# The last quarter of each low half, made by GpSimd in the last expert block

## The reference, cut to what matters

```
logits = xf @ router_w                       # (256, 8)
top_logit, top_idx = top_k(logits, 2); gates = softmax(top_logit)
# tokens sorted by expert into padded blocks of 128 rows
yb = (silu(xb @ w_gate[e]) * (xb @ w_up[e])) @ w_down[e]     # one block xb, expert e; w_gate (1024, 3584)
x  = x + sum over the token's two experts of yb[row] * gate
out = rms_norm(x)
```

## Time and profile before

| | us |
|---|---|
| median of 3 runs | 1396.18 (1395.97 to 1396.36) |
| the profiled execution, own time | 1393.4 |
| its span, first to last instruction | 1391.1 |
| TensorE busy | 1372.3 (99%) |
| VectorE busy | 1145.6 (82%) |
| ScalarE busy | 938.1 (67%) |
| GpSimd busy | 41.4 (3%) |
| HBM traffic over the span | 322 GB/s |
| `w_lo` instructions on VectorE (L390), 401 | 914.7 |

### The profile page before, as it was taken

The page is one execution under the profiler, slowest core; times in us unless marked ns, Lnnn a source line. Parts: engine busy times, 40 slices in busy tenths (PEclk is TensorE's granted clock), DMA queues, the critical chain, the costliest instruction groups (busy, mean ns, idle before and its releaser), DMA issues.

```text
span 1391.1 us, 19149 instructions
## 1 busy us (share of the span) xinstructions
PE 1372.3 (99%) x7313; PEld 1170.5 (84%) x7313; DVE 1145.6 (82%) x881; ACT 938.1 (67%) x759; POOL 41.4 (3%) x53
## 2 busy tenths in 40 slices
PE   9999999999999999999999999999999999999996
PEld 8888999889888888888888888888888888888875
DVE  6876575546867998888988888898888889889997
ACT  5565444444655777777777777777777777777776
POOL 0020000000010020000000000000000000000200
PEclk9999999999999999999999999999999999999999
DMA  9835985546425999999999999999999999999994
GB/s 334 281 110 159 406 307 187 204 155 211 152 92 191 347 376 393 396 393 397 385 395 390 360 386 382 381 369 389 394 350 397 393 369 376 391 392 351 398 393 170
DMA packets 191039, 448.80 MB, mean 323 GB/s; under 512 B 8515, under 2 KB 11274, under 8 KB 190986
## 3 DMA queue, kind: packets, MB, share of 16 engines
q1 hardware_dynamic: 189162, 441.74, 86.5%
q0 software_dynamic: 1616, 5.77, 1.1%
q10 hardware_dynamic: 208, 0.54, 0.1%
HBM read 429.67 MB, written 18.36 MB: 322 GB/s over the span
## 4 chain that ended last, share of the span: by engine, by line
PE 88%; DVE 7%; DMA 2%; issue 2%; ACT 1%; POOL 0%; DVEq 0%; ACTq 0%; POOLq 0%
PE ps L555 81%; DVE w_lo L390 4%; DMA raw<-in_expert_w_up 2%; PE ps L1017 2%; ACT w_hi L385 1%; PE ps L644 1%; PE ps L720 0%; PE ps L687 0%; PE ps L976 0%; PE ps L743 0%; PE ps L675 0%; DVE xs L1904 0%; PE ps L628 0%; PE ps L708 0%; PE ps L709 0%
## 5 line engine op out<-in xcount | busy, mean ns | idle before, releaser
L390 DVE TENSOR_TENSOR w_lo<-raw,w_hi 128x2048 fp32r<-128x2048 f32 x401 | 914.7, 2290 | 185.3 <-ACT w_hi L385 184.5
L385 ACT ACTIVATE w_hi<-raw 128x2048 fp32r<-128x2048 f32 x400 | 766.2, 1918 | 292.1 <-PE ps L555 280.3
L555 PE MATMUL ps<-w_hi,xe_hi 128*128 128x512 f32 x896 | 244.7, 395 | 0.6 <-DVE xe_lo L1910 0.6
L555 PE MATMUL ps<-w_hi,xe_lo 128*128 128x512 f32 x896 | 240.0, 390 | 0.0
L555 PE MATMUL ps<-w_lo,xe_hi 128*128 128x512 f32 x896 | 239.9, 389 | 0.0
L555 PEld LDWEIGHTS ps<-w_hi,xe_lo 128*128 128x128 f32 x896 | 168.2, 188 | 35.9
L555 PEld LDWEIGHTS ps<-w_lo,xe_hi 128*128 128x128 f32 x896 | 168.1, 188 | 35.5
L555 PEld LDWEIGHTS ps<-w_hi,xe_hi 128*128 128x128 f32 x896 | 164.6, 188 | 32.4 <-issue 0.8
L555 PE MATMUL ps<-w_lo,he_hi 128*128 128x512 f32 x448 | 122.0, 394 | 3.8 <-DVE w_lo L390 3.6
L555 PE MATMUL ps<-w_hi,he_hi 128*128 128x512 f32 x448 | 121.9, 393 | 0.5 <-ACT w_hi L385 0.5
L555 PE MATMUL ps<-w_hi,he_lo 128*128 128x512 f32 x392 | 104.8, 389 | 0.0
(11 more groups left out here) (271 smaller groups left out, 974.3 us busy)
## 6 DMA issues: line engine op xcount, KB each, us to landing
raw<-in_expert_w_gate SPq DMA_DIRECT2D x112, 1024.0 KB, 7.5
raw<-in_expert_w_up SPq DMA_DIRECT2D x112, 1024.0 KB, 7.6
raw<-in_expert_w_down SPq DMA_DIRECT2D x112, 1024.0 KB, 7.5
raw<-in_w_in SPq DMA_DIRECT2D x23, 1024.0 KB, 6.0
raw<-in_dense_w_gate SPq DMA_DIRECT2D x11, 1024.0 KB, 7.0
raw<-in_dense_w_up SPq DMA_DIRECT2D x11, 1024.0 KB, 7.8
raw<-in_dense_w_down SPq DMA_DIRECT2D x11, 1024.0 KB, 4.9
raw<-in_w_out SPq DMA_DIRECT2D x8, 1024.0 KB, 5.7
```

What stands on the lines that cost most here:

```text
L385: nc.scalar.activation(half_of(w_hi, n), raw[:, n % RAW, :], ACT.Copy).then_inc(hi_ready, 1)
L390: nc.vector.tensor_tensor(half_of(w_lo, n), raw[:, n % RAW, :], half_of(w_hi, n).bitcast(F32), ALU.subtract).then_inc(lo_ready, 1)
L555: return pe.matmul(o, stationary, moving, start=start, stop=stop, skip_group_check=True)
```

## The change

From g3.0 on (`SHARED`, the 17th piece), in the last block alone, VectorE makes the first 1536 columns of a piece's low half (`OWN`), and GpSimd the last 512 (`split_lo_end`), for 26 pieces. GpSimd counts them in a new semaphore, `lo_end_ready`. TensorE waits for it before the last matmul of a piece that reads those columns: the 12th of a gate or up piece, the 8th of a down piece. SyncE waits for it as well before it loads into the buffer. Nothing else is changed.

```diff
--- before.py
+++ after.py
@@ -59,6 +59,7 @@
 PER_BLOCK = 6 * E_CH
 MAX_BLOCKS = S * 2 // P + NE - 1
 FEW = P // 2
+OWN = PIECE - CH
 NEVER = 1.0e6
 ZERO_AT = 24
 Y_STORE, X_LOAD = 12, 32
@@ -265,6 +266,7 @@
 
         raw_in = [sem(f"raw_in{i}") for i in range(RAW)]
         hi_ready, lo_ready, piece_used = sem("hi_ready"), sem("lo_ready"), sem("piece_used")
+        lo_end_ready = sem("lo_end_ready")
         x_in = [sem("x_left"), sem("x_right")]
         first_in = sem("first_in")
         cst_in, small_in, lam_ld, bkt_in = (sem(n) for n in ("cst_in", "small_in", "lam_ld", "bkt_in"))
@@ -355,6 +357,7 @@
         ORDER = expert_pieces()
         assert len(ORDER) == PER_BLOCK and PER_BLOCK % RAW == 0 and PER_BLOCK % SPL == 0
         AT = {k: i for i, k in enumerate(ORDER)}
+        SHARED = AT[("gate", 3, 0)]
         ROUNDS = PER_BLOCK // RAW
 
         def landed(n, b=None):
@@ -384,11 +387,21 @@
                 act.wait_ge(piece_used, nth(n - SPL + 1, b))
             nc.scalar.activation(half_of(w_hi, n), raw[:, n % RAW, :], ACT.Copy).then_inc(hi_ready, 1)
 
-        def split_lo(dve, n, b=None):
+        def split_lo(dve, n, b=None, end=PIECE):
 
             dve.wait_ge(hi_ready, nth(n + 1, b))
-            nc.vector.tensor_tensor(half_of(w_lo, n), raw[:, n % RAW, :],
-                                    half_of(w_hi, n).bitcast(F32), ALU.subtract).then_inc(lo_ready, 1)
+            nc.vector.tensor_tensor(half_of(w_lo, n, 0, end), raw[:, n % RAW, 0:end],
+                                    half_of(w_hi, n, 0, end).bitcast(F32), ALU.subtract).then_inc(lo_ready, 1)
+
+        def split_lo_end(pool, n, b):
+
+            pool.wait_ge(hi_ready, nth(n + 1, b))
+            nc.gpsimd.tensor_tensor(half_of(w_lo, n, OWN), raw[:, n % RAW, OWN:PIECE],
+                                    half_of(w_hi, n, OWN).bitcast(F32), ALU.subtract).then_inc(lo_end_ready, 1)
+
+        def ends_made(i):
+
+            return i - SHARED + 1
 
         def x_slot(m, k):
 
@@ -409,9 +422,11 @@
                 sp.dma_start(first[:, 2:4, :], src[:, 2:4, :]).then_inc(raw_in[0], 16)
                 sp.dma_start(xs[:, :, CH:D], x_tiles[:, :, CH:D]).then_inc(x_in[1], 16)
 
-            def load(n, src, b=None):
+            def load(n, src, b=None, ends=0):
                 if n >= RAW:
                     sp.wait_ge(lo_ready, nth(n - RAW + 1, b))
+                if ends > 0:
+                    sp.wait_ge(lo_end_ready, ends)
                 dst = raw[:, n % RAW, :].rearrange("p (k n) -> p k n", n=src.shape[-1])
                 sp.dma_start(dst, src).then_inc(raw_in[n % RAW], 16)
 
@@ -466,7 +481,7 @@
                         src = edown_v[e, :, 4 * c + 2 * h:4 * c + 2 * h + 2, :]
                     else:
                         src = (egate_v if kind == "gate" else eup_v)[e, :, 4 * h:4 * h + 4, c * CH:c * CH + CH]
-                    load(MOE0 + i, src.rearrange("e p k n -> (e p) k n"), b)
+                    load(MOE0 + i, src.rearrange("e p k n -> (e p) k n"), b, ends_made(i - RAW) if last_block else 0)
 
             load_block(0, slice(0, 1), first=True)
             sp.wait_ge(tab_done, 1)
@@ -546,6 +561,9 @@
                 for t in range(TT):
                     pool.indirect_dma_start(y_of[:, i, t, :], None, y_rows,
                                             bass.IndirectOffsetOnAxis(ap=row_i[:, i, t:t + 1], axis=0)).then_inc(y_got[i][t], 16)
+
+            for i in range(SHARED, PER_BLOCK):
+                split_lo_end(pool, MOE0 + i, final)
 
 
         @block.tensor
@@ -996,6 +1014,11 @@
                 last.then_inc(sc_done[t], 1)
 
             def expert_block(b, first, last_block=False):
+                def low_end(kind, c, half):
+
+                    if last_block and ends_made(AT[(kind, c, half)]) > 0:
+                        pe.wait_ge(lo_end_ready, ends_made(AT[(kind, c, half)]))
+
                 def expert_in(kind, c, half):
                     n = MOE0 + AT[(kind, c, half)]
                     hi = high(n, b)
@@ -1008,6 +1031,8 @@
                         add(o, xe_lo[:, 4 * half + k, :], hi[:, k * CH:k * CH + CH])
                     lo = low(n, b)
                     for k in range(4):
+                        if k == 3:
+                            low_end(kind, c, half)
                         last = add(o, xe_hi[:, 4 * half + k, :], lo[:, k * CH:k * CH + CH], stop=(half == 1 and k == 3))
                     last.then_inc(piece_used, 1)
 
@@ -1048,6 +1073,8 @@
                     lo = low(n, b)
                     for f in range(2):
                         for o in range(2):
+                            if f == 1 and o == 1:
+                                low_end("down", c, half)
                             last = add(ps[:, 4 + o, :], he_hi[:, c % 2, 2 * half + f, :],
                                        lo[:, f * D + o * CH:f * D + o * CH + CH])
                     last.then_inc(piece_used, 1)
@@ -1925,8 +1954,9 @@
 
             def expert_block(b, first, last_block=False):
                 def lo_of(kind, c, half):
-                    if not (first and AT[(kind, c, half)] < SPL):
-                        split_lo(dve, MOE0 + AT[(kind, c, half)], b)
+                    i = AT[(kind, c, half)]
+                    if not (first and i < SPL):
+                        split_lo(dve, MOE0 + i, b, OWN if last_block and i >= SHARED else PIECE)
 
                 for c in range(E_CH + 1):
                     if c < E_CH:
```

## The result

The changed kernel takes 1400.41 us, median of 6 runs (1399.3 to 1401.65), against 1395.67 for the kernel before (1394.68 to 1396.36, 6 runs): a ratio of 1.0037, 95% interval 1.0026 to 1.0047. It is slower by 4.7 us, where 5.45 were forecast (1401.6, in a range from 1395.5 to 1410), and more than the 0.2% (2.8 us) that can be told from no change.

What follows compares the result with a forecast made beforehand. Landings plus some 2 us lost by VectorE bound the kernel; with the change, alternating turns set the pace. 4.95 us from turns and additions plus 0.5 for the clock, +5.45 on 1396.18, gave 1401.6 us, range 1395.5 to 1410.

Steps and rivals of the forecast that it cites:

- The turns: From g3.0 in the last block, GpSimd's and VectorE's low-half instructions exclude each other and alternate: a cycle of 2.765 us.
- the additions: Four additions of rows in chunks 4 and 5 take their turn in the same line: 2.6 us twice, 5.2.
- T: Time GpSimd needs after VectorE's end in each shared piece: taken as 1.15 us, from three masks.
- VectorE's part: Time VectorE needs after GpSimd's end in each shared piece: 0.02 + 1528 x 1.044 ns = 1.615 us.
- The sum: From g3.0's to d6.1's low half: 25 cycles, 69.1 us, plus 5.2; VectorE's last low half ends at 1381.5, +4.95.
- The base: Before the change, landings plus some 2 us lost by VectorE set the end; the forecast starts from the median, 1396.18.
- Two falls of the clock: TensorE's clock falls once more, at the second pair of additions of rows in the last block; counted as 0.5 us.
- B: Rival: both engines' low-half instructions run side by side and VectorE catches up, 2.8 us earlier: 1393.4; chance 0.07.
- C: Rival: not slower, GpSimd's turn is short; decides at T = 0.86, 1396.2 us; 1393.4 at T = 0.5; chance 0.16.

Runs made afterwards that it cites:

- The two misses of the kernel before: Kernel before with the last block's four additions of rows cut from 1024 columns to 8: 0.9996; kernel before with those additions moved apart: 1.0000.
- the kernel with the fill: The change with GpSimd subtracting only 8 of its 512 columns and filling 504 with zeros: 1392.8 us against 1395.5 before, ratio 0.9978.

## Why the prediction was right, and where it was off

**The turns.** Right, and shown from four sides: the instructions' spans, the reads taken away, the share's size, and the additions, which cost the same wherever they stand. T was taken as 1.15 us from three masks' time and is 1.16. VectorE's part was 1.615 and is 1.62. That T came so near is luck in part: it was counted by columns read and written, three times a mask's, and by that count the copy of 504 columns is two masks, 0.72 to 0.82 us, where it ended 0.46 after VectorE and took 0.60 whole.

The Trainium skill's price (GPSIMD Engine Reference, "Elementwise — side-by-side cycle accounting") gave 1.12 by estimate, a quarter of 4497 ns; the trace has 1.16 after VectorE's end and 1.30 for the whole instruction.

**The sum.** From the end of g3.0's low half to that of d6.1's the forecast had 69.1 + 5.2 = 74.3 us; the profile has 1384.08 - 1308.99 = 75.09. Before it was 1376.56 - 1307.72 = 68.84. So the change costs 6.25 us between these two marks, where 5.5 were forecast; at the very end VectorE waits 0.49 us for d6.1's high half, which the sum didn't have. The profiled spans differ by 7.5, since g3.0's low half ended 1.27 us later in the second one: that piece landed at 1305.18, not 1302.94, and the change doesn't touch it. From that landing to the end of down it is 81.52 us against 76.26, and so the change costs 5.26.

**The base.** The profiled execution went up by 7.0 us (1393.4 to 1400.38) and the median by 4.7, and this is where the forecast's reading was off. It says that "the end is set by the landings plus some 2 us that VectorE has lost". That was read from one execution, and not a usual one. With 1393.4 us it was as fast as the fastest of its kernel: of the 24 to 27 runs beside each group of experiments none was below 1393.42. Both its landing of g3.0 and its last landing were the earliest of all profiles. Two readings fit what followed:

- The usual execution differs only ahead of g3.0. Then the change costs the 5.26 us of the block. The medians of the spans bear this out, 1398.55 in the change's runs and 1393.1 to 1393.65 in those before, 4.9 to 5.45 apart. The rest is time outside the span, 1.8 us in the change's runs and 2.3 before, for which no run shows a reason.
- Where pieces land later, most of VectorE's lateness is hidden, and late landings cost the kernel before some 2 us of their own, while the line of turns no longer waits for them. The two misses of the kernel before speak for it (0.9996 and 1.0000 where 0.998 was due). Against it, the profile without additions is 2.4 us shorter than before from g3.0's landing on (73.84 against 76.26), as was expected.

No usual execution of the kernel before was profiled, so neither is shown, and why some runs land later no experiment here settled. The forecast's 5.45 lies near the 4.7 partly by luck: on the profiled execution it was 1.5 us short (1398.9 against 1400.38), and it was added to the median of executions unlike the one it was read from.

**The additions and the clock.** The additions were counted as 5.2 us in the line, whatever stands around them. Their two pairs last 7.8 us by the rows, and GpSimd's turns within them are part of that; the pieces behind are shorter for it (the low half at 1343.79 takes 1.75 us, as GpSimd's share of that piece was done). Two falls of the clock were forecast, and there was one in the block, after 4.28 us of idleness. Nothing in the rows answers to the 0.5 us counted for it, since VectorE's line was not held up. Taking the additions away from the change brought 0.22%, 3.1 us, where 5.2 were counted for them.

**The rivals.** B's mechanism fell, but its price, 2.8 us, is about what the kernel with the fill brought: 3 us, 0.9978, part of it from the shorter low halves at the very end. C's condition was a T below 0.86; the copy of one input is there with 0.46, the subtraction of two isn't.

## What to carry to other kernels

Before work is given to an engine that is idle in the profile, look for places where the two engines already meet, and at the spans there: four columns that take 1.89 us have waited for the other engine, and such waits turn shared work into a longer line. Set the cycle of that line against the pace of the stage: here the move cost 0 and 1.4 us below it, 5 and 23 above it. And read the gain that is to be had from more than one execution, since how late the stage's last transfer lands differs by more than such a gain.

## What the runs showed of the hardware

- Where both queue, GpSimd and VectorE took turns one instruction each, in the change and with 256 and 1024 columns. GpSimd's 8 columns ended 0.05 us after VectorE's low half (1311.75 to 1311.80), and VectorE's 8 columns 0.02 after GpSimd's mask.
- A GpSimd subtraction of two float32 inputs in SBUF held VectorE's two-input instructions for 0.05 us and 2.15 ns a column (8 to 1024 columns), a copy of 504 columns for 0.46 us. A fill of 504 columns in 0.52 us, with no read, stretched nothing.
- TensorE's granted clock fell to the 1.2 GHz level at waits of 2.44 us (before), 4.28 (the change), 3.07 (256 columns) and 2.17 (the change with the additions apart), and not at waits of 2.60 (8 columns), 2.42 (the change) or 2.19 (the change with the additions apart). With GpSimd behind VectorE it fell after 1.83 us, with 0.20 us of idleness and three matmuls just ahead of that; four matmuls took 1.7 us after it. The length of the last wait alone doesn't tell whether it falls.
